# The last 128 columns of each weight unit moved by 160 bytes, with four smaller changes of order and layout

## What is computed

```python
# first block
n = rmsnorm(h, g)
gq, gk, gv, gz, gb, ga, aq, ak, av, iq, ik, iw, gate_a, gate_b = split(n @ w_in)
y_gdn = gated_delta_branch(silu(conv4(gq, gk, gv)), ...)     # q and k are l2-normed
y_dsa = top_k_attention(aq, ak, av, iq, ik, iw)
merged = sigmoid(gate_a) * (y_gdn @ w_bg) + sigmoid(gate_b) * (y_dsa @ w_bd)
h = h + rmsnorm(merged @ w_out)
h = h + rmsnorm(square(relu(rmsnorm(h) @ w_up)) @ w_down)     # hidden width 4096
# second block
q, k, v, f, ga, gf = split(modulate(rmsnorm(x)) @ w_in2)      # k and v of a context too
heads = differential_attention(rope(q), rope(k), v)
y = sigmoid(ga) * (heads @ w_ao) + sigmoid(gf) * (fft(f).real @ w_fo)
x = x + g1 * (y @ w_out2)
x = x + g2 * mixture_of_16_experts(modulate(rmsnorm(x)))
return rmsnorm(x)
```

## Time and profile before

| | |
|---|---|
| timed runs | 1173.78 us median of 3 (1172.25 to 1173.88) |
| profiled execution, its own time | 1169.99 us |
| its span in the trace | 1168.2 us |
| PE busy | 1137.1 us, 97% |
| DVE, ACT, POOL busy | 668.7, 494.7, 84.7 us |
| instructions | 21501, of them 8980 matmuls |

### The profile page before, as it was taken

The page is one execution under the profiler, slowest core; times in us unless marked ns, Lnnn a source line. Parts: engine busy times, 40 slices in busy tenths (PEclk is TensorE's granted clock), DMA queues, the critical chain, the costliest instruction groups (busy, mean ns, idle before and its releaser), DMA issues.

```text
span 1168.2 us, 21501 instructions
## 1 busy us (share of the span) xinstructions
PE 1137.1 (97%) x8980; PEld 980.4 (84%) x8980; DVE 668.7 (57%) x1160; ACT 494.7 (42%) x777; POOL 84.7 (7%) x92
## 2 busy tenths in 40 slices
PE   9999999999999999999999999999999999999997
PEld 8998889998979989999979889767899866665664
DVE  7777966588776467775465342775656641221123
ACT  5775534635373655553535221667534311111112
POOL 2541320000000100000100000000001100000000
PEclk9999999999999999999999999999999999999999
DMA  9634330544415656555564322301956999999992
GB/s 368 226 144 181 109 146 1 176 150 144 181 38 181 254 219 251 184 208 186 190 244 190 114 93 73 145 2 62 355 213 256 379 418 423 424 426 424 424 427 90
DMA packets 36205, 254.61 MB, mean 218 GB/s; under 512 B 4048, under 2 KB 4192, under 8 KB 5904
## 3 DMA queue, kind: packets, MB, share of 16 engines
q1 hardware_dynamic: 33552, 237.84, 52.5%
q0 software_dynamic: 2560, 15.42, 3.3%
HBM read 252.19 MB, written 1.05 MB: 217 GB/s over the span
## 4 chain that ended last, share of the span: by engine, by line
PE 86%; DVE 9%; ACT 2%; issue 1%; DVEq 0%; ACTq 0%
PE bank L1427 15%; PE bank L727 12%; PE bank L721 12%; PE bank L722 12%; PE bank L1134 5%; PE bank L682 4%; PE bank L1220 4%; PE bank L1141 2%; PE bank L1439 2%; PE bank L1461 2%; PE bank L743 1%; PE bank L906 1%; DVE ring_low L2188 1%; PE bank L774 1%; PE bank L1246 1%
## 5 line engine op out<-in xcount | busy, mean ns | idle before, releaser
L2188 DVE TENSOR_TENSOR ring_low<-ring,w_high 128x2048 fp32r<-128x2048 f32 x104 | 238.0, 2290 | 148.8 <-ACT w_high L1698 148.8
L1698 ACT ACTIVATE w_high<-ring 128x2048 fp32r<-128x2048 f32 x104 | 199.1, 1916 | 279.0 <-PE bank L727 194.2
L721 PE MATMUL bank<-nT_high,w_high 128*128 128x256 f32 (+1 forms) x448 | 114.6, 296 | 0.0
L721 PEld LDWEIGHTS bank<-nT_high,w_high 128*128 128x128 f32 x448 | 84.5, 189 | 2.6 <-issue 2.4
L1427 PE MATMUL bank<-more,xs 128*64 128x256 f32 x768 | 84.5, 379 | 0.0
L1427 PEld LDWEIGHTS bank<-more,xs 128*64 128x64 f32 x768 | 55.0, 137 | 29.4 <-issue 2.3
L721 PE MATMUL bank<-hcl,w_high 128*128 128x256 f32 (+1 forms) x272 | 73.2, 306 | 0.0
L722 PE MATMUL bank<-hcl,w_high 128*128 128x256 f32 (+1 forms) x272 | 71.0, 298 | 0.0
L722 PE MATMUL bank<-nT_low,w_high 128*128 128x256 f32 (+1 forms) x272 | 64.6, 281 | 0.0
L721 PE MATMUL bank<-nMs,w_high 128*128 128x256 f32 x256 | 61.2, 284 | 0.0
L1134 PE MATMUL bank<-up,w_high 128*128 128x256 f32 x512 | 60.6, 276 | 0.0
(11 more groups left out here) (580 smaller groups left out, 2452.9 us busy)
## 6 DMA issues: line engine op xcount, KB each, us to landing
ring<-stream SPq DMA_DIRECT2D x163, 1024.0 KB, 5.1
more<-stream SPq DMA_DIRECT2D x60, 1024.0 KB, 18.9
more<-stream POOLq DMA_DIRECT2D x10, 1024.0 KB, 16.0
c<-constants_one SPq DMA_DIRECT2D x1, 1657.0 KB, 16.5
qc<-h_in SPq DMA_DIRECT2D x4, 272.0 KB, 3.5
c<-constants_two POOLq DMA_DIRECT2D x1, 1056.0 KB, 10.0
beside<-stream POOLq DMA_DIRECT2D x1, 1024.0 KB, 13.3
hT<-h_in POOLq DMA_DIRECT2D x1, 1024.0 KB, 6.0
```

Source lines behind the costliest of these rows:

```text
L721: nc.tensor.matmul(into[j], w, high_x(k), start=first, stop=False, skip_group_check=True)
L1698: A(w_high[:, d % 2, :], ring[:, s, :], ACT.Copy).then_inc(high_ready, 1)
L2188: TT(ring_low[:, s, :], ring[:, s, :], w_high[:, d % 2, :], sub).then_inc(low_ready, 1)
```

## The change

It has five parts.

1. `w_high` gets 64 words more per slot (2112 in place of 2048). The last 128 columns of a unit (block 15: `k` = 7, `j` = 1) lie 40 words, which is 160 bytes, further on than they would; the other 15 blocks stay. For `v2` the whole unit lies 32 words further on. ACT's copy and DVE's subtraction are therefore two instructions each (1920 and 128 columns) except for `v2`. Matmuls take their block from `high_block(d, i)`.
2. `_before_y_dsa_low` (32 words) is taken out. Behind the wider `w_high` all other tensors of that part move by 512 bytes, `y_dsa_low`, `aq`, `ak` and `y_dsa_high` by 384: those two start at 40 modulo 64 words where they started at 8.
3. `h_in` comes in 2 pieces in place of 4, ring slot 0 in two halves with a semaphore each; `wr` and `lam` are loaded behind POOL's other early DMAs.
4. `l2_sum(0)` and `l2_sum(1)` move from behind the unit of `t` = 4 into the middle of the unit of `t` = 6.
5. After the Exp for `lam`, ACT takes a Sqrt of one column into `warm`.

```diff
+HIGH_SLOT = KT * UNIT_COLS + 64
+LAST_BLOCK = KT * UNIT_COLS - 128
+LAST_SHIFT = 40
+HALF_UNIT = KT * UNIT_COLS // 2
...
-        w_high = sbr(dense, "w_high", 128, 2, KT * UNIT_COLS)
+        w_high = sbr(dense, "w_high", 128, 2, HIGH_SLOT)
...
-                _before_y_dsa_low = sb(m, "before_y_dsa_low", 128, HALF_LINE)
...
+        def high_pieces(d):
+
+            if SPLIT_UNITS[d][0] == "v2":
+                return [(w_high[:, d % 2, HALF_LINE:HALF_LINE + KT * UNIT_COLS], slice(0, KT * UNIT_COLS))]
+            return [(w_high[:, d % 2, 0:LAST_BLOCK], slice(0, LAST_BLOCK)),
+                    (w_high[:, d % 2, LAST_BLOCK + LAST_SHIFT:LAST_BLOCK + LAST_SHIFT + 128], slice(LAST_BLOCK, KT * UNIT_COLS))]
+
+        def high_block(d, i):
+
+            at = 128 * i + (LAST_SHIFT if 128 * i == LAST_BLOCK else 0)
+            return w_high[:, d % 2, at:at + 128]
...
-                        w = high_w[:, k, j * 128:(j + 1) * 128]
+                        w = high_block(d, 2 * k + j)
...
+                    def first_sums():
+
+                        if t == 6:
+                            l2_sum(0)
+                            l2_sum(1)
+
                     split_tiles(kind, u, lambda k: nT_high[:, k, :], lambda k: nT_rest[:, k, :], T, names,
-                                lambda k: pe.wait_ge(nT_rest_ready, k + 1) if t == 2 else None)
-                for i in range(12):
+                                lambda k: pe.wait_ge(nT_rest_ready, k + 1) if t == 2 else None, halfway=first_sums)
+                for i in range(2, 12):
...
-            for i in range(4):
-                sp.dma_start(qc[:, 2 * i:2 * i + 2, :], h_in[:, 2 * i:2 * i + 2, :]).then_inc(h_loaded[i], 16)
+            for i in range(2):
+                sp.dma_start(qc[:, 4 * i:4 * i + 4, :], h_in[:, 4 * i:4 * i + 4, :]).then_inc(h_loaded[i], 16)
             sp.dma_start(sm[:, :], sm_in).then_inc(sm_loaded, 16)
-            for s in range(SLOTS):
+            sp.dma_start(ring[:, 0, 0:HALF_UNIT], stream[0][:, 0:HALF_UNIT]).then_inc(first_half_loaded, 16)
+            sp.dma_start(ring[:, 0, HALF_UNIT:], stream[0][:, HALF_UNIT:]).then_inc(unit_loaded[0], 16)
+            for s in range(1, SLOTS):
...
-                    A(w_high[:, d % 2, :], ring[:, s, :], ACT.Copy).then_inc(high_ready, 1)
+                    for high, cols in high_pieces(d):
+                        ins = A(high, ring[:, s, cols], ACT.Copy)
+                    ins.then_inc(high_ready, 1)
...
                     A(lam[:, 6:8], full(act, "lam")[:, 0:2], ACT.Exp).then_inc(free("lam"), 1)
+                    A(warm[:, :], eps, ACT.Sqrt)
...
-                    TT(ring_low[:, s, :], ring[:, s, :], w_high[:, d % 2, :], sub).then_inc(low_ready, 1)
+                    for high, cols in high_pieces(d):
+                        ins = TT(ring_low[:, s, cols], ring[:, s, cols], high, sub)
+                    ins.then_inc(low_ready, 1)
```

More of the change, by code:

```diff
@@ L401, in build @@
         more_used = [sem(f"more_used{s}") for s in range(MORE)]
-        h_loaded = [sem(f"h_loaded{i}") for i in range(4)]
+        h_loaded = [sem(f"h_loaded{i}") for i in range(2)]
+        first_half_loaded = sem("first_half_loaded")
         c1_loaded, sm_loaded, ws_loaded = sem("c1_loaded"), sem("sm_loaded"), sem("ws_loaded")
@@ L663, in unit @@
                 at[0] += 1
-                pe.wait_ge(unit_loaded[s], 16 * n)
+                if at[0] == 1:
+                    pe.wait_ge(first_half_loaded, 16)
+                else:
+                    pe.wait_ge(unit_loaded[s], 16 * n)
                 return s, n
@@ L703, in split_unit @@
                 pe.wait_ge(high_ready, d + 1)
-                return s, cnt, d, [w.rearrange("p (k n) -> p k n", n=cols) for w in (w_high[:, d % 2, :], ring_low[:, s, :])]
+                return s, cnt, d, ring_low[:, s, :].rearrange("p (k n) -> p k n", n=cols)
             def low_parts(d):
@@ L1127, in _ @@
                 for kg in range(4):
-                    s, cnt, d, (high_w, low_w) = split_unit("down", cp * 4 + kg)
+                    s, cnt, d, low_w = split_unit("down", cp * 4 + kg)
                     if cp == 0:
@@ L1133, in _ @@
                             for part in range(2):
-                                nc.tensor.matmul(dst[:, j * SEQ:(j + 1) * SEQ], high_w[:, k, j * 128:(j + 1) * 128], up[:, kg * KT + k, part, :],
+                                nc.tensor.matmul(dst[:, j * SEQ:(j + 1) * SEQ], high_block(d, 2 * k + j), up[:, kg * KT + k, part, :],
                                                  start=(kg == 0 and k == 0 and j == 0 and part == 0), stop=False, skip_group_check=True)
@@ L1157, in keys_of_context @@
                         for part in (2, 3):
-                            nc.tensor.matmul(dst[j][:, SEQ:2 * SEQ], high_w[:, k, j * 128:(j + 1) * 128], hcl[:, part, k, :],
+                            nc.tensor.matmul(dst[j][:, SEQ:2 * SEQ], high_block(d, 2 * k + j), hcl[:, part, k, :],
                                              start=(k == 0 and part == 2), stop=False, skip_group_check=True)
@@ L1172, in keys_of_stream @@
                         for part in (0, 1):
-                            nc.tensor.matmul(dst[j][:, 0:SEQ], high_w[:, k, j * 128:(j + 1) * 128], hcl[:, part, k, :],
+                            nc.tensor.matmul(dst[j][:, 0:SEQ], high_block(d, 2 * k + j), hcl[:, part, k, :],
                                              start=False, stop=False, skip_group_check=True)
@@ L1215, in _ @@
             for u in range(4):
[L1216 removed]
+                s, cnt, d, low_w = split_unit("v2", u)
+                high_w = high_pieces(d)[0][0].rearrange("p (k n) -> p k n", n=UNIT_COLS)
                 dst = [take(("v2", u, tp)) for tp in range(2)]
@@ L1314, in _ @@
                         mod_unit(22 + u)
-                s, cnt, d, (high_w, low_w) = split_unit("fo", half, 512)
+                s, cnt, d, low_w = split_unit("fo", half, 512)
+                high_w = lambda i: high_block(d, i)
+                low_of = lambda i: low_w[:, i // 4, 128 * (i % 4):128 * (i % 4) + 128]
                 if half == 0:
@@ L1320, in four_by_weights @@
                 def four_by_weights(u, j, k, x, w, first=False, last=False):
-                    a = u * 256 + j * 128
-                    return nc.tensor.matmul(dst[u][:, j * SEQ:(j + 1) * SEQ], w[:, k, a:a + 128], x[:, k, :], start=first, stop=last, skip_group_check=True)
+                    return nc.tensor.matmul(dst[u][:, j * SEQ:(j + 1) * SEQ], w(4 * k + 2 * u + j), x[:, k, :], start=first, stop=last, skip_group_check=True)
                 for u in range(2):
@@ L1332, in _ @@
                         for k in range(4):
-                            last = four_by_weights(u, j, k, four_high, low_w, last=(k == 3))
+                            last = four_by_weights(u, j, k, four_high, low_of, last=(k == 3))
                     if u == 0:
@@ L1599, in _ @@
         def _(pool):
-            pool.dma_start(wr[:, :, :], wr_in).then_inc(small_loaded, 16)
-            pool.dma_start(lam[0:64, 0:4], lam_in).then_inc(small_loaded, 16)
             pool.wait_ge(nT_ready, KT)
@@ L1608, in _ @@
             pool.dma_start(ik_weights, ws_in[:, a:a + w].rearrange("p (k n) -> p k n", n=128)).then_inc(ws_loaded, 16)
+            pool.dma_start(wr[:, :, :], wr_in).then_inc(small_loaded, 16)
+            pool.dma_start(lam[0:64, 0:4], lam_in).then_inc(small_loaded, 16)
             for t in range(24):
```

21 lines of the change are left out of this document (12 added, 9 removed).

## The result

The changed kernel is slower: 1175.22 us in the median of seven runs (1173.3 to 1176.1) against 1171.27 us for the kernel before in seven runs on the same chip (1169.24 to 1173.88). The ratio is 1.0041, with a 95% interval of 1.0029 to 1.0052. The forecast was 1167.9 us and faster. The profiled execution took 1173.3 us, 3.3 us more than that of before.

What follows compares the result with a forecast made beforehand. PE, busy 97% of the span, was taken to bound the kernel. The terms, -5.0 + 0.5 - 0.4 + 0.3 - 1.3 = -5.9 us, took 1173.78 to 1167.9 us; the range over the cases was 1161.9, with 1 us to spare, to 1177.

Steps and rivals of the forecast that it cites:

- The two steps: 256-column matmuls on PE follow each other by 113.1 ns (short) or 117.5 ns (long), set when a stream starts anew.
- `v2`'s term: Moving the weights of the four long `v2` units makes them shorter: 0.9 us gained, bounds 0 and 1.8.
- The step that failed: Moved block in 256-column units turns long streams short and leaves short ones alone: 3.5 us gained, bounds 0 and 5.3.
- Rival C: Short streams turn long, the 28 units from 443.82 us at stake: 6.2 us more, 1179.1 us; chance 0.18.
- Rival B: Placement does nothing; the step is set at an interruption by timing alone: 1172.9 us; chance 0.16.
- the 24 of the prediction: Chain pieces of 16 low 256-column matmuls taking 1.88 to 1.90 us, from 222.19 to 895.36; 5.3 us at stake.
- Neither sign that the prediction named: Prediction is wrong if the step is a matter of timing alone, or if the stretch of 28 units starts long.
- 272 and 512 columns: Convolution and `k2` units might have a short step too, a guess: 0.6 us gained, bounds 0 and 3.9.
- The two instructions: Divided copy and subtraction on ACT and DVE, mostly hidden: +0.5 us, bounds 0.2 and 1.0.
- the l2 sums: Moved sums let the convolution's unit of `t` = 6 start without PE idling for the squares: 0.4 us gained.
- The first loads: At the start, halves delay the first squares, while the half ring slot removes a 0.23 us wait: +0.3 us, bounds -0.2 and +0.7.
- The root's table: Table load of 1.28 us ahead of the root at 599.84 us is taken out whole: -1.3 us.

Runs made afterwards that it cites:

- e3: Kernel before with only `v2`'s high weights moved 32 words, one instruction each for copy and subtraction: 1170.07 us against 1170.56, ratio 0.9995.
- e1: Changed kernel with block 15 back at its usual place, two instructions and all other parts kept: 1169.8 us against 1170.56 before, ratio 0.9987.
- e2: Kernel before with only block 15 moved 160 bytes, with two copies and two subtractions: 1176.84 us against 1170.56, ratio 1.0047.
- e5: Kernel before with only l2 sums 0 and 1 moved into the unit of `t` = 6: 1169.94 us against 1170.25, ratio 1.0002.
- e4: Kernel before with only the one-column Sqrt added behind the Exp for `lam`: 1169.15 us against 1170.56, ratio 0.9991.
- e9_without_loads: Changed kernel with the first loads as before, all the rest changed: 1173.41 us against 1170.61 before, ratio 1.0023.
- e13: Kernel before with blocks 0 and 1 at 40 words in all 93 split units behind the convolution but `v2`; `v2`, Sqrt, l2 sums changed: 1167.35 us, ratio 0.9974.
- e7_chosen: Kernel before with block 0 moved to 40 words in 11 chosen units, plus moved `v2` and added Sqrt: 1167.03 us against 1170.25, ratio 0.9977.
- e6_loads_alone: Kernel before with only the first loads changed (`h_in` in two pieces, ring slot 0 halved, `wr` and `lam` later): 1173.46 us against 1170.25, ratio 1.0038.

## Why the prediction was wrong

**The base.** The forecast took 5.9 us from 1173.78, the median of three runs; seven runs, these three among them, give 1171.27. The change was to bring -5.9 us and brought +3.95. So the change itself was missed by 9.9 us. That the time of 1175.2 lies only 7.3 us above the forecast is luck: the base came out 2.5 us lower. That it lies within the wide range of 1161 to 1177 says only how far the rivals lay apart.

**The two steps** were read rightly, and so was that PE's chain is where any gain or loss must show. `v2`'s term was right: 0.9 forecast, 1.1 in the trace, with the placement shown as its cause (e3). What it says of `y_dsa` is right too: at its new place the `bd` units are short (e1), which the moved block half undid.

**The step that failed** is "disturbs a long stream so that it falls into the short step, and leaves a short one alone". The second half is false for one block at 160 bytes. It turned nearly every 256-column unit over, both ways (e1 against e2, and 82 of 86 units after the change). Where streams were long that gained, but little: -0.5 us from 203 to 440 us, and -0.1 in e2, where `y_dsa` had not moved. Where they were short it lost: +3.3 in the one stretch of 28 units, +1.25 from 731 us on. The term was -3.5 us and is +4.0. Rival C had the stretch and the sign, but as one bad start, with all units long (+6.2); half of each unit is. Rival B is excluded by e1 against e2. What spoke against me stood in my own argument: the only evidence for a disturbance was one change from long to short, and I had no case of a short stream disturbed. Before the change 54 of the 86 low parts are short and 32 long (the 24 of the prediction are those that the chain shows as one piece of 16); after it 43 and 43. A disturbance that works both ways costs more than it brings there, and I gave it no case of its own. Neither sign that the prediction named for its being wrong came: the step is not a matter of timing alone (e1, e2), and the stretch of 28 units started short.

**272 and 512 columns** (-0.6) never changed: 0.

**The two instructions** (+0.5) and **the l2 sums** (-0.4): +0.6 in the convolution, which is 0.5 above the +0.1 of the two terms, and for another reason. In its own trace the moved sums have -0.8, a part of it perhaps chance (e5). Where nothing collides the second instruction costs ACT 0.09 us, as estimated, and DVE 0.07 (2.36 for 2.29 us), but 0.64 us a pair in the convolution, where POOL's multiply comes in between them. PE's waits for a subtraction stayed at 2.7 us in all, as forecast. I had counted PE's waits for a subtraction, and not who shares time with DVE.

**The first loads** (+0.3): 0 in this trace (the first unit starts 0.4 us earlier, the third, at 23.6 us, 0.05 later), since the sums ran at full speed from the second matmul on; in two other traces of the same loads the start is 1.2 and 1.7 us later than before. The estimate took PE's speed there as given.

**The root's table** (-1.3): -0.8. The load is gone, but the ring load behind it then ends the wait (e4). That was mis-sized because I followed the chain only from the root to its user and did not ask what arrives next.

The terms as measured in the trace: blocks with `y_dsa` +4.0, `v2` -1.1, start and convolution +0.6, table -0.8, the stretch of lower clock +0.6; together +3.3, the difference of the two profiled executions. In the timed medians the difference is +3.95, and by the ratio 4.8. What the loads add in the timed runs is open (e9_without_loads).

**What stays open.** Why the step goes by the places of the operands modulo 256 bytes and by the number of matmuls read from the moved place. That a pattern of four matmuls is left in its middle by two, and at its end by four or sixteen, fits all the traces with short streams; for long streams in e13 it doesn't suffice. No run moves the activations alone. The two cases that were long at their old place and short at the new one, `bd` and the high part of `v2`, both had the moving operand 16 words further on than the stationary one modulo 64, and then 16 words less; that this is the rule is not shown, since `up` and `q2` units have the second distance too and are long in places, and one `v2` unit of e6_loads_alone is short at the old place.

## What to carry to other kernels

Where a kernel holds one of two speeds and a change disturbs it, ask what the disturbance does to either state, and weigh it by how much time is spent in each; a fix that flips the state belongs only where the state is bad (one block in 11 chosen units brings some 1.0 us in e7_chosen; one block in every unit costs 0.47%). Look at the places of both operands: moving `y_dsa`, a by-product of the change, gained more in e1_no_offset (1.3 us) than those 11 blocks. An instruction that is cut in two costs more than its fixed part when another engine waits for it to end (0.64 us in place of 0.07): look at who runs beside it. For a wait that is removed, read off what arrives next before booking the whole of it.

## What the runs showed of the hardware

- Matmuls of 256 columns back to back take 113 or 118 ns. The state survives from unit to unit (28 units on end), can change at an interruption (437.78 to 443.82 in the earlier trace rows), and changes when an operand comes from another place modulo 256 bytes. For the weights: 2 matmuls at 160 bytes turn it over (82 of 86 units), 4 or 16 leave a short stream short, 2 at 32 bytes leave it short and turn a long one short in most places (21 of 26), and 256 bytes do nothing. For the activations: the `bd` units are long in 14 traces with `y_dsa` at 8 words and short in 3 with it at 40, and a stream changes at the border to such a unit (e3). With the weights as the moving side (`v2`) 32 words more make the 64 high matmuls short, in 26 of 28 units. The Trainium skill ("SBUF — State Buffer", Who interferes with whom) gives PE two read ports, one for each operand, independent of each other. That doesn't explain a step that depends on where one operand lies; here the measurement decides.
- DVE's subtraction of two SBUF tensors and POOL's multiply hold each other up: POOL's 0.77 us becomes 2.3 to 2.6 beside an undivided subtraction, and a divided one takes 0.64 us more.
- PE's f32 matmuls of 272 columns take 450 ns at the start of the kernel, and 225 ns from a moment on that varies from the first sum to 10.5 us between executions; after a pause of 1.0 us the four traces show only early (none slow, or the first at most) and late (9 and 11 slow). The clock's records begin where the 450 ns end, and the windows view counts the time ahead of them as 1.00.
- In single stretches of a few microseconds the granted clock is 0.50 (922.7 to 926.1 us after the change), at places that change from execution to execution and cost 0.6 to 2.2 us each.
